# Output projections in 512-column weight tiles over half of the contraction, two banks per token block

## The chip, the cores and the metric

The kernel runs on one core of one Trainium2 chip. The metric is the device time of one launch in microseconds. Three runs of the kernel before gave 2868.2, 2872.81 and 2876.31 us, median 2872.81.

## What is computed

Four transformer layers over 512 tokens of width 1024, all in float32. The first two are a dilated window mixer and a differential attention mixer; the last two are each a hybrid mixer (indexer-selected attention beside gated linear attention) and a feed-forward network with a convolution of width 3. Cut to what matters here:

```
def dilated_mixer(h, w_in, w_out):          # layer 1; diff_mixer, layer 2, ends the same way
    ...
    y = o.reshape(B, S, DIL_WIDTH).astype(h.dtype) * jax.nn.silu(gate)
    return y @ w_out                        # 512x1024 @ 1024x1024: l1o, l2o

def hybrid_mixer(x, pos, ...):
    ik = partial_rope(ik[:, :, None, :], pos)[:, :, 0, :]      # the keys' rope
    ...
    merged = jax.nn.sigmoid(gate_a) * ya + jax.nn.sigmoid(gate_b) * yb
    return merged @ w_out + b_out           # m0o, m1o

def conv_ffn(x, w_up, conv_w, conv_b, w_down):
    ...
    return (jax.nn.gelu(a) * b) @ w_down    # contraction 2816 = 1024 + 1024 + 768: d0, d1, d2

h = h + rmsnorm(y, norm_post[i])            # first two layers: "resid"
x = layer_norm(DN_ALPHA * x + y, g, b)      # hybrid and feed-forward: "ln"
```

## The kernel before

**Split operands.** Every float32 operand of a projection is held as two fp32r parts, high and low, and a product is three matmuls: high x high, high x low, low x high. A weight tile arrives by DMA in one of two raw buffers (`WR`), in two halves; ScalarE writes its high part (step `split`, L1897) and POOL subtracts it for the low part in four pieces (step `lo`, L2821; the very first tile is done by VectorE in two). A tile is loaded when the low part of the tile two before it is done. The parts lie in one of three ring slots (`WS`), or, for the third tile of an output projection, in a fourth slot `EX`.

**Tiles.** 214 tiles are used in a fixed order. A name tells the stage (`l1`, `l2`: the first two layers; `m0`, `m1`: the hybrid mixers; `f0`, `f1`: the feed-forward networks) and the projection. "Token-major" products have the activations (in `UT` or `AT`) as stationary operand (L1552, "WS,UT" and so on); "feature-major" ones have the weights (L1549). The wide input projections use pairs of tiles of 512 columns, each over half the contraction (`-` marks the first half). The output projections `l1o`, `l2o`, `m0o`, `m1o` and the last part `f0d2`, `f1d2` use four tiles of 256 columns over the whole contraction (8 or 6 blocks of 128).

**One order for all engines.** The class `Order` writes out, ahead of the run, one list of steps; every engine walks that list in order and does its own part of each step, so each engine's queue has the order of the list. `fill(n)` puts the `split` steps of the tiles below n there, `tick` counts matmul steps: each tick pops one waiting `lo` and lets steps planned with `soon` (turns, ropes, splits) come when their count is over. `turn` is the transpose of one block of 128 tokens (TensorE, then ScalarE's high part and VectorE's low part); `wide(..., fresh=True)` is the first projection after a seam, which forces the turns it needs.

**The output projections.** `by_blocks` walks the four token blocks. Block 0 is opened by hand (list `opening`) while the last gates are transposed in chunks, and has four banks; the others have two banks of which each tile fills half. After a block its epilogue step follows: `resid` (ScalarE squares, VectorE, POOL's rstd, VectorE) or `ln` (VectorE, with POOL's rstd at L2836). The order is block by block, all four tiles in each. Then the next stage starts: `l2a0` after `l1o`, `m0iq` after `l2o` and `m1iq` after `f0d2` (both begin at token block 1), the feed-forward network's convolution table and its first pair after `m0o` and `m1o`.

**At a tile.** A product step waits, before its first matmul in the first block, for both halves of the high part and the whole low part.

Of the kernel before, what the change touches and what calls it, by code (L numbers as in the profile page):

```python
# [9 lines left out]
ALU = mybir.AluOpType  # L10
# [80 lines left out]
def weight_tiles(ap):  # L91
# [9 lines left out]

    out = []
# [9 lines left out]
    for j in range(4):  # L112
        out.append((f"l1o{j}", KC, 256, [(0, cols(ap["dil_w_out"][0], 256 * j))]))
# [6 lines left out]
    for j in range(4):  # L120
        out.append((f"l2o{j}", KC, 256, [(0, cols(ap["diff_w_out"][0], 256 * j))]))
    for l in range(2):
# [18 lines left out]
        for j in range(4):  # L141
            out.append((f"m{l}o{j}", KC, 256, [(0, cols(ap["w_mix_out_2"][l], 256 * j))]))
        for kind, j in ffn_order():
# [4 lines left out]
            elif j < 2:  # L148
                for c in range(2):
                    wide(f"f{l}d{j}{c}", ap["w_down_2"][l], 512 * c, r0=j * 1024)  # L150
            else:
                for c in range(4):
                    out.append((f"f{l}d{j}{c}", 6, 256, [(0, cols(ap["w_down_2"][l], 256 * c, k=6, r0=j * 1024))]))
# [19 lines left out]
class Order:  # L173
# [103 lines left out]
    def by_pool(self, i):  # L277

        return i > 0
# [56 lines left out]
    def wide(self, name, deal, by=1, fresh=False, hold=lambda: False, first=0):  # L336
# [42 lines left out]
    def by_blocks(self, names, finish, opening, order=(0, 1, 2, 3)):  # L379
# [3 lines left out]
        more = i0 + 4 < len(self.tiles)  # L383
        for b in range(NB):
            split = b == 0
            banks = (order, (4, 5), (0, 1), (2, 3))[b]
            for n, what in enumerate(opening if split else ()):
                if n == 2:
                    self.fill(i0 + 3)
                elif n == 4:  # L390
# [3 lines left out]
                else:  # L394
# [6 lines left out]
            for j in range(4):  # L401
                if len(ws) == j:
                    ws.append(self.open(names[j]))
                if not split or j == 3:
                    self.bank[ws[j], b] = (banks[j], 0) if split else (banks[j // 2], 256 * (j % 2))
                    self.step("mm", ws[j], b, 0, self.tiles[ws[j]][1])
                if b == 3 and j < LOOK and more and self.place[i0 + 4] < NS:
# [3 lines left out]
                if b == 1 and j < LOOK and more and self.place[i0 + 4] > NS:  # L411
# [2655 lines left out]
```

## Time and profile before

| | us |
|---|---|
| median of three runs | 2872.81 |
| the profiled execution | 2872.07 |
| its span, first to last instruction | 2870.8 |
| TensorE busy | 2765.1 |
| VectorE busy | 1196.3 |
| ScalarE busy | 1096.9 |
| POOL busy | 1115.2 |

The mean granted TensorE clock is 0.99 of full speed. PE is TensorE's matmuls, PEld its weight loads, DVE VectorE, ACT ScalarE, SP the queue that issues the DMAs. A row of the timeline says when a group of instructions began, how long it lasted, and in brackets how long the engine was idle before it and what ended that; the chain of work is followed back from the last instruction.

### The profile page before, as it was taken

What the parts mean: (1) busy time and instruction counts of PE and PEld (TensorE: products, weight loads), DVE (VectorE), ACT (ScalarE), POOL (GpSimd) and SP (SyncE); (2) the same over time, 40 slices, a digit from 0 to 9 for tenths busy, and PEclk for the clock granted to TensorE, in tenths of its full rate; (3) what the DMA queues carried; (4) which work ended last, traced back from release to release, by engine and by line L of the source; (5) the groups of instructions that cost most, each with busy time, mean ns of one, the idle gap of its engine ahead of it and who ended that gap; (6) DMA issues with size and microseconds to landing.
All of it is one profiled execution on the core that took longest, in us unless ns stands there. A gap on an engine that the chain in (4) does not pass through costs nothing.

```text
span 2870.8 us, 39675 instructions
## 1 busy us (share of the span) xinstructions
PE 2765.1 (96%) x15257; PEld 2278.5 (79%) x15257; DVE 1196.3 (42%) x2661; ACT 1096.9 (38%) x2045; POOL 1115.2 (39%) x902
## 2 busy tenths in 40 slices
PE   6999999998999999999999999989999999999998
PEld 5787878888878977776789888887777678988887
DVE  3333433344455355433335424255643433542425
ACT  3444434443455334362323424233436232342421
POOL 3323233334343343332355444434333235444443
PEclk9999999999999999999999999999999999999999
DMA  5332323232222142223253323224222324333331
GB/s 160 93 93 73 90 82 87 77 101 86 74 66 67 55 135 74 74 85 110 65 173 112 103 89 102 90 60 135 74 74 85 111 72 169 109 103 95 96 92 55
DMA packets 252670, 269.04 MB, mean 94 GB/s; under 512 B 16830, under 2 KB 214050, under 8 KB 251716
## 3 DMA queue, kind: packets, MB, share of 16 engines
q1 hardware_dynamic: 252484, 266.51, 30.4%
q8 instruction: 122, 2.00, 0.3%
q14 instruction: 64, 0.52, 0.1%
HBM read 247.52 MB, written 18.94 MB: 93 GB/s over the span
## 4 chain that ended last, share of the span: by engine, by line
PE 88%; DVE 6%; ACT 3%; issue 2%; POOL 1%; DMA 0%; SPq 0%; DVEq 0%; ACTq 0%; POOLq 0%
PE banks L1552 46%; PE banks L1549 27%; DVE AR L2239 2%; PE banks L1686 2%; PE banks L1570 2%; PE banks L1635 1%; PE banks L1793 1%; POOL WS L2821 1%; PE banks L1669 1%; PE banks L1706 1%; ACT WS L1897 1%; PE banks L1841 1%; PE banks L1609 1%; PE banks L1757 1%; PE banks L1654 1%
## 5 line engine op out<-in xcount | busy, mean ns | idle before, releaser
L2821 POOL TENSOR_TENSOR WS<-WR,WS 128x512 fp32r<-128x512 f32 (+2 forms) x812 | 1014.5, 1283 | 1460.7 <-ACT WS L1897 1460.7
L1552 PE MATMUL banks<-WS,UT 128*128 128x512 f32 (+1 forms) x5712 | 1210.5, 361 | 15.1 <-issue 7.0
L1552 PEld LDWEIGHTS banks<-WS,UT 128*128 128x128 f32 x5712 | 913.2, 190 | 190.5 <-issue 55.9
L1549 PE MATMUL banks<-UT,WS 128*128 128x512 f32 (+1 forms) x2832 | 667.8, 394 | 0.7 <-ACT AR L2072 0.7
L1549 PEld LDWEIGHTS banks<-UT,WS 128*128 128x128 f32 (+1 forms) x2832 | 528.6, 188 | 125.6 <-issue 15.4
L1897 ACT ACTIVATE WS<-WR 128x1024 fp32r<-128x1024 f32 (+2 forms) x408 | 396.0, 1021 | 203.3 <-PE banks L1552 151.2
L1552 PE MATMUL banks<-WS,AT 128*128 128x256 f32 (+1 forms) x1776 | 307.9, 334 | 13.1 <-issue 11.4
L1552 PEld LDWEIGHTS banks<-WS,AT 128*128 128x128 f32 x1776 | 267.9, 192 | 49.0 <-issue 12.1
L2239 DVE TENSOR_TENSOR AR<-AR 128x256 f32<-128x256 f32 (+2 forms) x173 | 157.5, 929 | 12.0 <-ACT AR L2140 7.2
L2761 DVE SCALAR_TENSOR_TENSOR AR<-banks,AR 128x511 f32<-128x511 f32 x84 | 63.0, 750 | 219.2 <-ACT AR L2208 219.2
L2836 POOL TENSOR_TENSOR SM<-SM 128x1 f32<-128x1 f32 (+2 forms) x44 | 47.0, 1069 | 275.5 <-DVE SM L2737 111.4
L2239 DVE TENSOR_TENSOR AR<-banks,CT 128x256 f32<-128x256 f32 (+1 forms) x168 | 71.9, 479 | 121.0 <-ACT AR L1965 64.9
L1951 ACT ACTIVATE AR<-banks 128x256 f32<-128x256 f32 (+1 forms) x118 | 59.3, 559 | 152.6 <-PE banks L1635 152.6
L2239 DVE TENSOR_TENSOR AR<-AR,banks 128x512 f32<-128x512 f32 (+1 forms) x72 | 43.6, 626 | 175.1 <-PE banks L1552 174.3
L2341 DVE CUSTOM_DVE_ANT_0 AF<-banks,MF 128x256 f32<-128x256 f32 (+1 forms) x128 | 47.0, 404 | 167.0 <-PE banks L1654 117.3
L2208 ACT ACTIVATE AR<-banks,AR 128x512 f32<-128x512 f32 x84 | 65.0, 774 | 87.9 <-PE banks L1549 81.7
L1549 PE MATMUL banks<-AT,WS 128*128 128x512 f32 x384 | 88.2, 391 | 0.0
L1549 PEld LDWEIGHTS banks<-AT,WS 128*128 128x128 f32 x384 | 72.1, 188 | 15.8
L1918 ACT ACTIVATE UT<-banks 128x512 fp32r<-128x512 f32 x48 | 26.2, 595 | 149.8 <-PE banks L1609 149.8
L2218 ACT ACTIVATE AT<-AR 128x512 fp32r<-128x512 f32 x40 | 25.3, 632 | 108.8 <-DVE AR L2239 108.8
L1686 PEld LDWEIGHTS banks<-AR,AF 128*128 128x128 f32 x480 | 61.7, 191 | 4.3 <-issue 0.7
L1984 ACT ACTIVATE AF<-banks 128x512 f32<-128x512 f32 (+1 forms) x64 | 36.7, 573 | 73.9 <-PE banks L1669 73.9
(220 smaller groups left out, 2647.0 us busy)
## 6 DMA issues: line engine op xcount, KB each, us to landing
WR<-in_w_in SPq DMA_DIRECT2D x112, 512.0 KB, 3.6
WR<-in_w_up SPq DMA_DIRECT2D x88, 512.0 KB, 3.6
WR<-in_dil_w_in SPq DMA_DIRECT2D x256, 128.0 KB, 2.5
WR<-in_w_down SPq DMA_DIRECT2D x32, 512.0 KB, 3.3
WR<-in_dil_w_in SPq DMA_DIRECT2D x16, 512.0 KB, 4.4
WR<-in_diff_w_in SPq DMA_DIRECT2D x32, 256.0 KB, 3.0
WR<-in_diff_w_in SPq DMA_DIRECT2D x16, 512.0 KB, 3.7
spill<-AR SPq DMA_DIRECT2D x32, 256.0 KB, 2.1
```

Source lines behind the costliest of these rows:

```text
L1549: mm = pe.matmul(B[bank][0:c, :], w[x][:, kk, g * P:g * P + c], act[:, y, kk, :], start=start, stop=stop)
L1552: mm = pe.matmul(B[bank][:, off:off + n], act[:, x, before_k + kk, g * P:g * P + P], w[y][:, kk, :], start=start, stop=stop)
L1570: mm = pe.matmul(B[c][:, 256 * half:256 * half + 256], w[x][:, kk, (c % 2) * P:(c % 2) * P + P], UT[:, y, kk, 256 * half:256 * half + 256] ...
L1686: mm = pe.matmul(B[ob][:, r:r + 64], fat(7168 + 512 * e + 256 * hh + j * P, P), vj, start=(j == 0), stop=(j == w // P - 1))
L1897: se.activation(slot(i, 0)[:, v * h:v * h + h], raw(i)[:, v * h:v * h + h], ACT.Copy).then_inc(hi.sem, 1)
L1951: se.activation(d, s, ACT.Copy).then_inc(pair_out.sem, 1)
L2208: se.activation(d, B[order.bank[i, half][0]][:, :], ACT.Identity, scale=cp[:, 2, f:f + 1], bias=cp[:, 3, f:f + 1]).then_inc(conv_id.sem, 1)
L2239: return ve.tensor_tensor(out_, x, y, op)
L2341: x = ve.tensor_tensor_reduce(P1(e, hh, w), B[4 + hh][:, 0:w], MF[:, 256:512] if far else MF[:, 256 - w:256], -0.125, -GONE, ALU.add, ALU. ...
L2761: ve.scalar_tensor_tensor(d[:, 1:T], bank[:, 0:T - 1], cp[:, 1, f:f + 1], d[:, 1:T], ALU.mult, ALU.add).then_inc(dve_step, 1)
L2821: ge.tensor_tensor(slot(i, 1)[:, s], raw(i)[:, s], slot(i, 0)[:, s].bitcast(F32), ALU.subtract).then_inc(lo_p.sem, 1)
L2836: ge.tensor_tensor(SM[:, o:o + n], SM[:, o:o + n], SM[:, MHALF:MHALF + n], ALU.pow).then_inc(rstd.sem, 1)
```

## The change

1. The output projections' tiles (`joined`) are 512 columns wide over 4 blocks of the contraction: tiles 0 and 1 are the first half, for the left and right columns, tiles 2 and 3 the rest (4 blocks, or 2 in `d2`). Each token block has two banks, block 0 too, and each bank collects two tiles.
2. `by_blocks` has a new order: block 0, block 1, then tiles 0 and 1 of blocks 2 and 3 (`(2,0),(3,0),(2,1),(3,1)`), then tiles 2 and 3 of block 2, its epilogue, tiles 2 and 3 of block 3, its epilogue. The third and fourth tiles are split before the first and second part of the opening; in `d2` the splits come around the last feature tile, and `d2`'s fourth tile gets its low part from VectorE.
3. Every product step makes its three passes one after another over its blocks of the contraction (weights high by activations high, high by low, then low by high), and waits for each half of the tile by itself: for the high half before, for the low half only before the third pass.
4. The partial rope (`part`, `small_tokens`) takes 4 VectorE instructions instead of 6, and the keys' rope 4 instead of 24 for its four blocks.
5. `m0iq` and `m1iq` alternate the two tile halves from token block 1 on.
6. At the start x's first block, the gain and the identity are loaded ahead of the first weight tile, x's second block behind it, and the second tile is split before x's third block is normalised.

```
+    def joined(name, w, r0=0, rest=4):
+        for half, k in enumerate((4, rest)):
+            for c in range(2):
+                out.append((f"{name}{2 * half + c}", k, 512, [(0, cols(w, 512 * c, 512, k=k, r0=r0 + 512 * half))]))
...
-        return i > 0
+        return i > 0 and self.tiles[i][0][2:] != "d23"
...
-            walk = [(half, b) for half in range(2) for b in (first, first + 1)]
-            walk += [(half, b) for b in range(first + 2, NB) for half in range(2)]
+            both = first + 2 if first == 0 else first
+            walk = [(half, b) for half in range(2) for b in range(first, both)]
+            walk += [(half, b) for b in range(both, NB) for half in range(2)]
...
-    def by_blocks(self, names, finish, opening, order=(0, 1, 2, 3)):
+    def by_blocks(self, names, finish, opening, first=(0, 1)):
...
+        banks_of = (first, (4, 5), (0, 1), (2, 3))
+        walk = [[], [(1, j) for j in range(4)],
+                [(2, 0), (3, 0), (2, 1), (3, 1), (2, 2), (2, 3)], [(3, 2), (3, 3)]]
...
-                if n == 2:
+                if n == 0:
                     self.fill(i0 + 3)
-                elif n == 4:
+                elif n == 2:
                     self.fill(i0 + 4)
...
-                    self.bank[ws[j], b] = (banks[j], 0)
+                    self.bank[ws[j], b] = (banks[j % 2], 0)
                     self.step("mm", ws[j], b, k0, k1)
-                    self.tick()
+                    self.tick((k1 - k0) // 2)
+            for g, j in walk[b]:
+                self.bank[ws[j], g] = (banks_of[g][j % 2], 0)
+                self.step("mm", ws[j], g, 0, self.tiles[ws[j]][1])
...
-        parts = [(0, 0, 4), (1, 0, 4), (0, 4, 6), (1, 4, 6), (2, 0, 6), (0, 6, 8), (1, 6, 8), (2, 6, 8)]
-        for n, what in enumerate(turns):
-            parts.insert(2 * n, what)
+        parts = [(0, 0, 4), (1, 0, 4), (2, 0, 2), (3, 0, 2), (2, 2, 4), (3, 2, 4)]
+        for n, what in zip((0, 2, 3, 5), turns):
+            parts.insert(n, what)
...
+            if b == 1:
+                self.fill(2)
...
                 i = self.open(f"f{l}b10")
+                self.fill(i + 4)
...
+                self.fill(i + 5)
...
-        self.by_blocks([f"f{l}d2{c}" for c in range(4)], finish, [(j, 0, 6) for j in range(3)], order=(2, 3, 0, 1))
+        self.by_blocks([f"f{l}d2{c}" for c in range(4)], finish,
+                       [(0, 0, 4), (1, 0, 4), (2, 0, 2), (3, 0, 2)], first=(2, 3))
...
+                    fetched = 0 if 2 * last <= k else 1
+                    opens = g == order.first_block.get(i, 0) and (first == 0 or 2 * first == k)
+                    if opens:
+                        pe.wait_ge(hi.sem, hi.at[i, fetched])
                     if first == 0:
-                        if g == order.first_block.get(i, 0):
-                            pe.wait_ge(hi.sem, hi.at[i, 1])
-                            pe.wait_ge(*lo_done(i))
...
-                    for kk in range(first, last):
-                        for q, (x, y) in enumerate(PASSES):
+                    for part, other in ((0, 0), (0, 1), (1, 0)):
+                        if part and opens:
+                            pe.wait_ge(*lo_done(i, fetched))
+                        for kk in range(first, last):
...
-                    for b in range(nb):
-                        x1, x2 = y[:, b, :, 0:8], y[:, b, :, 8:16]
...
-                        tt(q[0], x1, cs, ALU.mult)
-                        tt(q[1], x2, sn, ALU.mult)
-                        tt(q[2], x2, cs, ALU.mult)
-                        tt(q[3], x1, sn, ALU.mult).then_inc(dve_step, 1)
...
+                    tt(xc, x, cs.unsqueeze(2).to_broadcast([P, n, 2, 8]), ALU.mult)
+                    tt(xs, x, sn.unsqueeze(2).to_broadcast([P, n, 2, 8]), ALU.mult).then_inc(dve_step, 1)
+                    ve.wait_ge(dve_step, V.of())
+                    tt(x[:, :, 0, :], xc[:, :, 0, :], xs[:, :, 1, :], ALU.subtract)
+                    tt(x[:, :, 1, :], xc[:, :, 1, :], xs[:, :, 0, :], ALU.add).then_inc(done.sem, 1)
...
-            load_tile(0)
-            sy.dma_start(fat(2048, D), whole(ap["norm_pre"][0])).then_inc(gain_in, 16)
             x_by_rest = ap["x"][0].rearrange("(l r) d -> r l d", r=4)
             sy.dma_start(x_at[:, 0, :], x_by_rest[0]).then_inc(x_in[0], 16)
+            sy.dma_start(fat(2048, D), whole(ap["norm_pre"][0])).then_inc(gain_in, 16)
             sy.dma_start(IDN, tab[:, C_ID:C_ID + 128]).then_inc(id_in, 16)
-            for b in range(1, NB):
+            load_tile(0)
+            sy.dma_start(x_at[:, 1, :], x_by_rest[1]).then_inc(x_in[1], 16)
+            load_tile(1)
+            for b in range(2, NB):
```

## Rows read from the trace of the kernel before

**Rows 1.** The page's head and its busy times.

```profile
span 2870.8 us, 39675 instructions
...
PE 2765.1 (96%) x15257; PEld 2278.5 (79%) x15257; DVE 1196.3 (42%) x2661; ACT 1096.9 (38%) x2045; POOL 1115.2 (39%) x902
```

**Rows 2.** Chain of work: start us, us, what and how many.

```profile
978.96 11.06 PE banks L1552 x96
...
1542.67 11.47 PE banks L1552 x96
...
1657.87 44.80 PE banks L1552 x192
...
2513.36 76.18 PE banks L1549 x336
```

**Rows 3.** Timeline, the start: start us, us, engine, line [idle before].

```profile
13.40 1.06 ACT L1910 ACTIVATE AF<-AF 128x1024 f32<-128x1024 f32 x1 [11.39 <-DMA AF<-in_x]
...
16.99 1.94 PE L1609 MATMUL banks<-CT,AR 128*128 128x128 f32 x8 [16.99 <-DVE AR L2269]
...
19.46 1.99 ACT L1897 ACTIVATE WS<-WR 128x1024 fp32r<-128x1024 f32 x2
...
23.00 2.90 PE L1552 MATMUL banks<-WS,UT 128*128 128x512 f32 x6 [4.07 <-DVE WS L2239]
...
39.42 9.81 PE L1552 MATMUL banks<-WS,UT 128*128 128x512 f32 x42 [0.19 <-DVE UT L2239]
```

**Rows 4.** Timeline, openings of l1o, l2o, m0o and f0d2.

```profile
646.01 0.97 PE L1552 MATMUL banks<-WS,AT 128*128 128x256 f32 x6 [1.26 <-DVE AT L2239]
...
958.75 2.39 PE L1552 MATMUL banks<-EX,AT 128*128 128x256 f32 x18 [0.91 <-issue]
...
1514.88 8.86 PE L1552 MATMUL banks<-WS,UT 128*128 128x256 f32 x72 [0.87 <-issue]
...
1896.29 1.56 ACT L1897 ACTIVATE WS<-WR 128x768 fp32r<-128x768 f32 x2
...
1901.14 7.04 PE L1552 MATMUL banks<-WS,AT 128*128 128x256 f32 x36 [5.16 <-issue]
```

**Rows 5.** Timeline, the seam from l1o to l2a0.

```profile
689.56 10.92 POOL L2821 TENSOR_TENSOR WS<-WR,WS 128x512 fp32r<-128x512 f32 x8
...
691.99 1.09 PE L1609 MATMUL banks<-CT,AR 128*128 128x128 f32 x8 [0.98 <-DVE AR L2269]
...
695.62 12.54 PE L1552 MATMUL banks<-WS,UT 128*128 128x512 f32 x48 [2.53 <-issue]
...
700.43 0.56 POOL L2836 TENSOR_TENSOR SM<-SM 128x1 f32<-128x1 f32 x1
...
714.26 0.63 PE L1635 MATMUL banks<-CT,AR 128*128 128x128 f32 x4 [3.84 <-DVE UT L2239]
714.64 4.59 PE L1552 MATMUL banks<-WS,UT 128*128 128x512 f32 x12
```

**Rows 6.** Timeline, the keys' rope in the first hybrid mixer.

```profile
1030.20 3.94 DVE L2239 TENSOR_TENSOR SM<-AR 128x8 f32<-128x8 f32 x4 [6.59 <-ACT AR L2084]
...
1041.02 1.06 PE L1747 MATMUL banks<-CT,AR 128*64 128x128 f32 x4 [3.12 <-DVE AR L2239]
1041.73 5.31 PE L1552 MATMUL banks<-WS,UT 128*128 128x512 f32 x12
```

**Rows 7.** Timeline, the seam from f0d2 to m1iq.

```profile
1930.51 2.25 DVE L2745 SCALAR_TENSOR_TENSOR AR<-AR,SM 128x1024 f32<-128x1024 f32 x1 [0.51 <-POOL SM L2836]
...
1936.43 11.42 PE L1552 MATMUL banks<-WS,UT 128*128 128x512 f32 x42 [2.53 <-issue]
```

**Rows 8.** Timeline, the convolution table after m0o.

```profile
1556.08 0.41 PE L1865 MATMUL banks<-CT,AR 44*128 44x44 f32 x4 [1.07 <-DVE UT L2239]
```

**Rows 9.** Timeline, VectorE after the last matmul.

```profile
2862.77 0.69 DVE L2239 TENSOR_TENSOR AR<-AR,banks 128x512 f32<-128x512 f32 x1 [2.38 <-PE banks L1552]
```

**Rows 10.** Busy times of a stretch; the granted clock is PEclk.

```profile
core 0: us, PE busy (x) PEld busy (x) DVE busy (x) ACT busy (x) POOL busy (x), PEclk, DMA share, GB/s
1900.00:1908.00 8.00, 6.86 (x36) 6.89 (x37) 2.57 (x6) 0.00 (x0) 1.55 (x3) 0.57 0.40 131
```

More of the change, by code:

```diff
@@ L111, in weight_tiles @@
         out.append((f"l1g{j}", KC, 256, [(0, cols(w, 9216 + 256 * j))]))
-    for j in range(4):
-        out.append((f"l1o{j}", KC, 256, [(0, cols(ap["dil_w_out"][0], 256 * j))]))
+    joined("l1o", ap["dil_w_out"][0])
     w = ap["diff_w_in"][0]
@@ L119, in weight_tiles @@
         out.append((f"l2g{j}", KC, 256, [(0, cols(w, 3072 + 256 * j))]))
-    for j in range(4):
-        out.append((f"l2o{j}", KC, 256, [(0, cols(ap["diff_w_out"][0], 256 * j))]))
+    joined("l2o", ap["diff_w_out"][0])
     for l in range(2):
@@ L140, in weight_tiles @@
             out.append((f"m{l}pg{j}", KC, 256, [(0, cols(ap["p_gla_2"][l], 256 * j))]))
-        for j in range(4):
-            out.append((f"m{l}o{j}", KC, 256, [(0, cols(ap["w_mix_out_2"][l], 256 * j))]))
+        joined(f"m{l}o", ap["w_mix_out_2"][l])
         for kind, j in ffn_order():
@@ L151, in weight_tiles @@
             else:
-                for c in range(4):
-                    out.append((f"f{l}d{j}{c}", 6, 256, [(0, cols(ap["w_down_2"][l], 256 * c, k=6, r0=j * 1024))]))
+                joined(f"f{l}d{j}", ap["w_down_2"][l], r0=j * 1024, rest=2)
     return out
@@ L397, in by_blocks @@
                         ws.append(self.open(names[j]))
-                    self.bank[ws[j], b] = (banks[j], 0)
+                    self.bank[ws[j], b] = (banks[j % 2], 0)
                     self.step("mm", ws[j], b, k0, k1)
-                    self.tick()
[L401 to L407, printed above, removed]
+                    self.tick((k1 - k0) // 2)
+            for g, j in walk[b]:
+                self.bank[ws[j], g] = (banks_of[g][j % 2], 0)
+                self.step("mm", ws[j], g, 0, self.tiles[ws[j]][1])
+                if g == 3 and j < LOOK and more and self.place[i0 + 4] < NS:
                     self.limit += 1
@@ L1525, in tensor @@
                             pe.wait_ge(*before[i, g])
[L1526 removed]
+                    before_k = 4 if is_second(i) else 0
+                    if g == 0 and grouped[i]:
                         if name[:3] in ("l1o", "l2o"):
[L1528 removed]
+                            pe.wait_ge(chunk_lo.sem, chunk_lo.at[name[:2] + "g", before_k + last - 1])
                         elif name[0] == "m":
[L1530 to L1531 removed]
+                            pe.wait_ge(merge_lo.sem, merge_lo.at[int(name[1]), before_k + last - 1])
+                        elif before_k == 0:
                             pe.wait_ge(prod_lo.sem, prod_lo.at[int(name[1]), 9, 1])
@@ L1534, in tensor @@
                             pe.wait_ge(prod_lo.sem, prod_lo.at[int(name[1]), 10, 1, 0])
-                    if g == 2 and name[:4] in ("f0d2", "f1d2"):
+                    if g == 2 and grouped[i] and name[0] == "f" and is_second(i):
                         pe.wait_ge(prod_lo.sem, prod_lo.at[int(name[1]), 10, 1, 1])
```

71 lines of the change are left out of this document (27 added, 44 removed).

## The prediction

> **What bounds the kernel now.** I read the page first. TensorE is busy 96% of a span of 2870.8 us [rows 1], and no other engine comes near it. So only two things can move the time: how long one matmul takes, and the stretches in which TensorE stands still or runs at half clock. The idle left over is 105.7 us (2870.8 less 2765.1).
>
> The chain of work that ended last gives the matmul's price in dense stretches [rows 2]. A feature-major tile costs 76.18/336 = 0.2267 us per 512-column matmul; a token-major one whose stationary operand lies in AT costs 44.80/192 = 0.2333. The 256-column matmuls of the output projections cost 11.06/96 = 0.1152 us (stationary in AT, `l1o`) and 11.47/96 = 0.1195 (in UT, `m0o`). These are close to streaming time; there is nothing large to win in them.
>
> Then the timeline around every seam between two stages, where the bracket behind a PE row is its idle. The seams are: the start [rows 3], the openings of the six output projections [rows 4], the end of `l1o` into `l2a0` [rows 5], the keys' rope in the hybrid mixer [rows 6], `f0d2` into `m1iq` [rows 7], the convolution table [rows 8] and the tail [rows 9]. Behind the long idles the granted clock falls: 0.57 over 1900 to 1908 [rows 10], which is the lower of the two levels, 1.2 GHz, for most of the stretch. So an idle of 3 to 5 us is paid again in part.
>
> **The change, part by part.**
>
> *Wider matmuls.* 4 x 384 + 2 x 288 = 2112 matmuls of 256 columns become 1056 of 512. One token block (a quarter of a projection): `l1o`, `l2o`: 11.06 becomes 48 x 0.2333 = 11.20, +0.14, eight blocks +1.1. `m0o`, `m1o`: stationary in UT, where the 512-column price is nearest 0.2267: 11.47 becomes 10.88, eight blocks -4.7. `f0d2`, `f1d2`: 72 x 0.1152 = 8.29 becomes 36 x 0.2333 = 8.40, eight blocks +0.9. Sum **-2.7**. Were the price 0.2333 everywhere it would be 0; were it 0.2267 everywhere -7. The Trainium skill ("TensorE: Matmul & The Clock Gate", Back-to-back issue gap) gives N/2.4 + 2.5 ns for one isolated matmul; by that two of 256 cost 218.3 ns and one of 512 costs 215.8, and the whole would be an estimated -2.6 us. The rows say 230 to 239 against 227 to 233, so they keep the sum but not the sign in every stage.
>
> *Openings.* Block 0 now starts with four chunks in two banks, the third and fourth tiles are split earlier, and each half of a tile is waited for by itself, the low part only before the third pass. `l1o` idles 1.26 (waiting for a chunk's low part), `l2o` 0.91, `m0o` 0.87 (`m1o` repeats it) [rows 4]; three more idles like these, of 0.53, 0.44 and 0.52, lie beside them in `l1o` and `l2o`. In `l1o` ScalarE's two splits, 2.0 us each, now stand ahead of the chunk copies; I leave 0.6 us of idle in each. Gain 1.8 + 1.9 - 1.2 = 2.5, and 2 x 0.9 = 1.8 for `m`. For `f0d2` ScalarE splits the fourth tile only at 1896.29, POOL's four subtractions follow, and TensorE idles 5.16 us until 1901.14; then 36 matmuls take 7.04 instead of 36 x 0.1152 = 4.15, because the clock is low: 2.9 more [rows 4, 10]. After: the fourth tile (half as large per row) is split as soon as the last feature tile is done, its low part is on VectorE (0.7 us per half, as for the 512-wide addition of [rows 9]), and TensorE needs it 7 us (24 + 6 matmuls) after the opening. I leave 0.4. Gain 2 x (4.8 + 2.9) = 15.4. Together **-19.7**.
>
> *Seam `l1o` to `l2a0`.* TensorE idles 0.98 (a normalised block for the transposes), 2.53 (low part of the first tile; POOL subtracts from 689.56 to 700.48) and 3.84 (the rope of `l2a0`, late because POOL's rstd of block 3, which ends the previous stage, was queued behind those subtractions until 700.43) [rows 5]. At half clock 48 matmuls took 12.54 instead of 10.88 and 12 took 4.59 instead of 2.72: 3.5 us. Now the first two tiles of the projection end 16.8 and 11.2 us before its last matmul, so the next tiles' splits and subtractions (2.0 and 5.2 us each) are over before the seam, and rstd is not behind them. Blocks 2 and 3 finish only 24 matmuls = 5.6 us apart instead of 11; VectorE needs about 3 + 1.3 + 1.3 us a block, so block 3 is turned in time for its use 11 us into `l2a0`. Full gain 10.9; I take **-10**, and -5 for the range if the rope still waits.
>
> *Keys' rope.* 24 small VectorE products start at 1030.20 (the first four take 3.94 us) and end with the wait of TensorE, which idles 3.12 us until 1041.02 and then pays 5.31 for 12 matmuls instead of 2.72 [rows 6]; the second layer repeats it with 2.39 and 4.49 - 2.72 = 1.77. Four products with the blocks joined remain. They took 10.8/24 = 0.45 us each; at that they end 9 us earlier. At 1.4 us each (one POOL subtraction, 10.92/8 = 1.37 [rows 5], in front of every one) they still end at 1036, before TensorE asks at 1037.9. **-9.9.** The Trainium skill ("SBUF — State Buffer", SBUF: two separate sides) says a VectorE instruction with two SBUF inputs and a GpSimd one exclude each other for a whole instruction; the trace agrees in kind (four products spread over 3.94 us while POOL subtracts), and by it the bound is this same 1.4 us a piece.
>
> *Convolution table.* Its transposes come right after `m0o`'s last block, whose turn used to hold the bank. 1.07 idle in each of two layers [rows 8] goes: **-1.9** (rounded down by the switch).
>
> *The start.* x's first block is issued behind eight weight loads and a gain and reaches ScalarE at 13.40; the transposes start 3.6 us after that, the split of the tile at 19.46, the first product at 23.0; the fourth block's last stretch at 39.42 [rows 3]. After: x is first, so it lands near 5; the gain bounds the product, transposes near 8.5; the tile lands near 10.5, the first product near 12. Then blocks 2 and 3 of x come behind two weight tiles; ScalarE's order (norms 0, split, norm 1, split, norms 2 and 3, turn 1) puts block 1's turn near 22 instead of 30, and the same 4.1 us per block follow. **-8**; bounds -3 (bound by the loads) and -12.
>
> *What it costs.* In `m1iq` the walk starts at block 1 and alternates halves, so block 2's turn is needed after 24 matmuls and 8 transposes, 6.6 us after the seam. In VectorE's queue that turn's low part stands behind both `ln` of blocks 2 and 3, which now finish only 12 matmuls = 2.8 us apart. One `ln` is two additions (0.69 [rows 9], overlapping a little), two statistics of 0.64, 0.36 for two small ones, a product of 1.28, 0.5 of waiting for rstd and a last product of 1.28, or 2.25 beside POOL [rows 7]: 6 to 7 us. So: block 2 from -2.8 to +3, block 3 to +9.5, low part to +10.8: a new idle of 3.2 to 5.2, with half clock behind it (1.7) and 0.8 for a second late turn. It replaces 2.53 + 1.9 [rows 7]. **+2.0**. In `m0iq` the residual is shorter, only the second turn shows: **+0.8**. At the end VectorE does block 3 behind block 2: from the last matmul at 2862.7 it now takes about 8.4 instead of 5.3 us to the output: **+2.9** [rows 9].
>
> Sum: -2.7 - 19.7 - 10 - 9.9 - 1.9 - 8 + 2.0 + 0.8 + 2.9 = **-46.5**. The profiled execution took 2872.07 (span 2870.8 and 1.3 around it), 0.7 below the median 2872.81. So 2825.6 for such an execution, **2826** for the median.
>
> **Rivals.**
> - *A. The waits move, half the gain stays* (0.14). Two banks per block mean blocks 2 and 3 end together, and VectorE and ScalarE get their epilogues in a heap. If that costs an idle of 4 us with low clock in `l2a0` and `m0iq` too, and the start gains only 3: 2826 + 5 + 6 + 5 + 4 = 2846. For it: VectorE's queue in [rows 7]. Against: residual blocks are shorter than `ln`.
> - *B. More than I count* (0.12). The low part's later wait also helps wherever a split is late, and the start gains 12: 2808 to 2816. Against: the other waits of TensorE are for ropes and exponentials.
> - *C. Slower: the added waits break the stream* (0.04). 208 tiles get three more places at which TensorE waits in the middle of an accumulation: 624. If each opened a gap of 0.1 us, as long as the step from a 256-column product to another kind of operation shows (0.20 instead of 0.12 us in the records), it costs 62 us: 2888. It decides from 74 ns each. Against: 336 matmuls over seven tiles, with waits at each tile and bank, stay at 0.2267 [rows 2].
> - *D. No change: the new order of passes* (0.03). Now each product loads another stationary block, where before two of three shared one. If 6400 matmuls went from 0.2267 to 0.2333: +42 us, about 2868. Against: the shared and the unshared third are in the same 0.2267, 13 ns above 512/2.4.
> - My forecast: 0.67.
>
> The forecast's own range is 2816 to 2836; with A and B it is 2808 to 2848, which leaves out C, D and tails. No change means within 0.3% (8.6 us), which is about what can be told here. Faster 0.94, same 0.02, slower 0.04.
>
> **What would show it.** TensorE's first 512-column product near 12 us and the long run at 39.42 some 8 us earlier; no idle over 1.5 us at the opening of `f0d2` and `f1d2`; none before `l2a0` and the keys' transposes, and no fall of the clock there; a wait on VectorE's turn of 3 to 5 us in `m1iq`; last matmul to end of span 11 us instead of 8.3; 512-column products of `m0o` at 0.227 and of `l1o` at 0.233. I am wrong if dense stretches change their price, if the idle at the seams comes back under VectorE's name, or if the first tile is held up by the loads.

## The result, and the profile after

The changed kernel took 2833.82 us (median of four runs, 2832.68 to 2834.95) against 2870.51 for the kernel before beside it (2867.95 to 2876.31): ratio 0.9869, 95% interval 0.9852 to 0.9887. Between the two profiled executions the span went from 2870.8 to 2831.4 us, **39.4 less**; 46.5 were forecast. Line numbers of kernel.py have moved: L1552 is now L1562, L1549 is L1559, L1609 is L1619, L1635 is L1645, and VectorE's L2239 is L2249. In the kernels of the experiments the same lines have moved by a few more.

The head of the page, against [rows 1]: TensorE is busy 13.4 us less, and its idle has gone from 105.7 to 79.7 us.

```profile
span 2831.4 us, 37369 instructions
...
PE 2751.7 (97%) x14201; PEld 2220.0 (78%) x14201; DVE 1181.5 (42%) x2569; ACT 1095.8 (39%) x2037; POOL 1112.0 (39%) x894
```

The chain of work, against [rows 2]: the dense stretches have not changed their price by a hundredth. New are the 512-column products of the output projections, 16.71/72 = 0.2321 in `l1o` and 22.04/96 = 0.2296 in `m0o`.

```profile
643.73 16.71 PE banks L1562 x72
...
1486.00 22.04 PE banks L1562 x96
...
1560.09 76.18 PE banks L1559 x336
1636.27 44.80 PE banks L1562 x192
```

The following table compares the moments at which the same tile's first matmul starts in the two traces. Each line is the change in us of the distance between two such moments. The forecast's terms are grouped to the same places: of the 2.5 us for the openings, 1.2 stand at `l1o` and 1.3 at `l2o`, and of the matmuls' +1.1, half at each.

| from - to | forecast | measured |
|---|---|---|
| start to the second tile (the second half of `l1a0`) | -8.0 | -5.3 (42.3 to 36.9) |
| `l1o` to `l2v0`: opening, seam | -10.7 | -6.5 (86.2 to 79.7) |
| `l2o` to `m0ik` | 0.0 | -1.8 (71.3 to 69.5) |
| the keys' rope, two layers | -9.9 | -10.2 |
| `m0o`, `m1o` to the feed-forward network | -8.4 | -4.2 (76.2 to 74.1, twice) |
| `f0d2` to `m1ik`: opening, seam | -5.2 | -6.7 (67.9 to 61.2) |
| `f1d2` to the last matmul | -7.2 | -7.9 |
| last matmul to the end | +2.9 | +3.1 (8.3 to 11.5) |
| everywhere else | 0 | 0 (within 0.1) |
| sum | -46.5 | -39.5 |

Timeline, the start, against [rows 3]: the first product comes at 12.37 instead of 23.00, as forecast, but then TensorE stands 3.26 us for VectorE's low part of block 1, and works at the lower level of the clock, 1.2 GHz, behind it (6 matmuls in 2.93 us; the granted clock from 24.4 to 27.3 is 0.50).

```profile
12.37 2.93 PE L1562 MATMUL banks<-WS,UT 128*128 128x512 f32 x6 [1.63 <-ACT WS L1907]
...
23.05 1.27 DVE L2249 TENSOR_TENSOR UT<-banks,UT 128x512 fp32r<-128x512 f32 x2
24.38 2.93 PE L1562 MATMUL banks<-WS,UT 128*128 128x512 f32 x6 [3.26 <-DVE UT L2249]
```

Timeline, the seam from `l1o` to `l2a0`, against [rows 5]: of the three idles the first two are gone (TensorE runs through from 684.31), POOL's rstd of block 3 is on time (687.34, ahead of the subtractions of 692.85), and yet the third idle is there as before, 3.85 us, with 9 matmuls in 3.64 us behind it. VectorE's rows say why. What TensorE waits for is named UT, the low part of the turn of block 3 (701.58). It stands in VectorE's queue behind the ropes of blocks 0 and 1, which write AR; the sums of the first rope take 2.56 us beside POOL's subtractions, those of the second 0.76.

```profile
687.34 0.55 POOL L2835 TENSOR_TENSOR SM<-SM 128x1 f32<-128x1 f32 x1 [1.72 <-DVE SM L2460]
...
692.85 6.25 POOL L2820 TENSOR_TENSOR WS<-WR,WS 128x512 fp32r<-128x512 f32 x4 [0.21 <-ACT WS L1907]
...
695.45 1.34 DVE L2249 TENSOR_TENSOR AR<-banks,CT 128x512 f32<-128x512 f32 x3
696.82 2.56 DVE L2249 TENSOR_TENSOR AR<-AR 128x256 f32<-128x256 f32 x2
699.52 1.35 DVE L2249 TENSOR_TENSOR AR<-banks,CT 128x512 f32<-128x512 f32 x3
700.90 0.76 DVE L2249 TENSOR_TENSOR AR<-AR 128x256 f32<-128x256 f32 x2
701.58 1.28 DVE L2249 TENSOR_TENSOR UT<-banks,UT 128x512 fp32r<-128x512 f32 x2
...
696.14 1.03 PE L1619 MATMUL banks<-CT,AR 128*128 128x128 f32 x8
696.93 1.64 PE L1562 MATMUL banks<-WS,UT 128*128 128x512 f32 x6
702.41 0.63 PE L1645 MATMUL banks<-CT,AR 128*128 128x128 f32 x4 [3.85 <-DVE UT L2249]
```

Timeline, the keys' rope, against [rows 6]: two products and two sums in 3.9 us instead of 24 instructions in 10.8; TensorE reaches the transposes at 1024.18 with no idle and a full clock behind (12 matmuls in 2.99).

```profile
1016.63 1.49 DVE L2249 TENSOR_TENSOR SM<-AR 128x64 f32<-128x64 f32 x2 [6.74 <-ACT AR L2094]
1018.15 2.44 DVE L2249 TENSOR_TENSOR AR<-SM 128x32 f32<-128x32 f32 x2
...
1024.18 0.60 PE L1757 MATMUL banks<-CT,AR 128*64 128x128 f32 x4
```

Timeline, behind `m0o`, against [rows 8]: the convolution table comes without a wait, but a new idle of 1.86 us follows. It ends with L2750, VectorE's copy of the table, which frees a bank; that copy is queued behind the `ln` of block 3 (its last product takes from 1537.78 to 1539.99).

```profile
1531.70 0.44 PE L1875 MATMUL banks<-CT,AR 44*128 44x44 f32 x4
...
1539.92 0.33 DVE L2750 COPY AR<-banks 128x176 f32<-128x176 f32 x1
1540.30 0.66 PE L1619 MATMUL banks<-CT,AR 128*128 128x128 f32 x4 [1.86 <-DVE AR L2750]
```

Timeline, the opening of `f0d2`, against [rows 4]: no idle. And the seam into `m1iq`, against [rows 7]: the forecast wait for a turn, 4.17 us, and 18 matmuls in 5.99 us instead of the 4.28 that they take at 1903.31.

```profile
1867.83 5.77 PE L1562 MATMUL banks<-WS,AT 128*128 128x512 f32 x24
1873.44 1.54 PE L1562 MATMUL banks<-EX,AT 128*128 128x512 f32 x6
1874.91 7.26 PE L1562 MATMUL banks<-WS,AT 128*128 128x512 f32 x30
...
1903.31 4.28 PE L1562 MATMUL banks<-WS,UT 128*128 128x512 f32 x18
...
1914.03 5.99 PE L1562 MATMUL banks<-WS,UT 128*128 128x512 f32 x18 [4.17 <-DVE UT L2249]
```

Timeline, VectorE in the tail, against [rows 9]: block 3's `ln` starts when block 2's ends (2822.80), not when its own products do.

```profile
2821.59 1.28 DVE L2744 SCALAR_TENSOR_TENSOR AR<-AR,SM 128x1024 f32<-128x1024 f32 x1 [0.51 <-POOL SM L2835]
2822.80 1.28 DVE L2249 TENSOR_TENSOR AR<-AR,banks 128x512 f32<-128x512 f32 x2
```

The granted clock, against [rows 10]: 0.79 on the mean of the two stretches of 8 us around the idles that stay, that is, the lower level for some 3.4 of the 8 us (an estimate from 0.79, with the levels at 0.5 and 1).

```profile
core 0: us, PE busy (x) PEld busy (x) DVE busy (x) ACT busy (x) POOL busy (x), PEclk, DMA share, GB/s
...
700.00:708.00 8.00, 5.59 (x22) 4.58 (x23) 2.83 (x7) 0.75 (x2) 0.00 (x0) 0.79 0.22 68
1912.00:1920.00 8.00, 5.97 (x20) 4.75 (x21) 2.93 (x7) 0.00 (x0) 2.23 (x3) 0.79 0.79 286
```

### The profile page after: what moved, and what is told of

It is laid out like the page before. It is cut to its first block, busy times and chain, and to the rows that moved or that the text cites. A ratio compares the mean times of both kernels' runs of the same rounds, so it can differ in the third digit from the quotient of the medians.

```text
span 2831.4 us, 37369 instructions
## 1 busy us (share of the span) xinstructions
PE 2751.7 (97%) x14201; PEld 2220.0 (78%) x14201; DVE 1181.5 (42%) x2569; ACT 1095.8 (39%) x2037; POOL 1112.0 (39%) x894
## 4 chain that ended last, share of the span: by engine, by line
PE 89%; DVE 5%; ACT 2%; issue 2%; POOL 1%; SPq 0%; DMA 0%; DVEq 0%; ACTq 0%
PE banks L1562 47%; PE banks L1559 27%; PE banks L1696 2%; DVE AR L2249 2%; PE banks L1645 1%; PE banks L1580 1%; PE banks L1803 1%; PE banks L1679 1%; PE banks L1595 1%; PE banks L1716 1%; PE banks L1851 1%; POOL WS L2820 1%; PE banks L1664 1%; PE banks L1767 1%; PE banks L1781 1%
## 5 line engine op out<-in xcount | busy, mean ns | idle before, releaser
L1562 PE MATMUL banks<-WS,UT 128*128 128x512 f32 (+1 forms) x5424 | 1204.5, 370 | 10.3 <-DVE UT L2249 8.6
L1562 PEld LDWEIGHTS banks<-WS,UT 128*128 128x128 f32 x5424 | 894.8, 190 | 195.7 <-issue 43.5
L1559 PE MATMUL banks<-UT,WS 128*128 128x512 f32 (+1 forms) x2832 | 668.7, 395 | 0.7 <-ACT AR L2082 0.7
L1559 PEld LDWEIGHTS banks<-UT,WS 128*128 128x128 f32 (+1 forms) x2832 | 529.5, 189 | 125.6 <-issue 15.4
L1907 ACT ACTIVATE WS<-WR 128x1024 fp32r<-128x1024 f32 (+1 forms) x408 | 396.9, 1023 | 210.2 <-PE banks L1562 167.7
L1562 PE MATMUL banks<-WS,AT 128*128 128x512 f32 x1296 | 308.2, 396 | 0.0
L1562 PEld LDWEIGHTS banks<-WS,AT 128*128 128x128 f32 x1296 | 242.6, 188 | 58.4 <-ACT WS L1907 0.7
L2249 DVE TENSOR_TENSOR AR<-AR 128x256 f32<-128x256 f32 (+2 forms) x173 | 156.0, 920 | 12.0 <-ACT AR L2150 7.2
L2249 DVE TENSOR_TENSOR AR<-banks,CT 128x256 f32<-128x256 f32 (+1 forms) x168 | 71.9, 479 | 121.0 <-ACT AR L1975 61.7
L2249 DVE TENSOR_TENSOR AR<-AR,banks 128x512 f32<-128x512 f32 x64 | 43.0, 685 | 167.1 <-PE banks L1562 165.8
L1559 PE MATMUL banks<-AT,WS 128*128 128x512 f32 x384 | 88.2, 391 | 0.0
L1559 PEld LDWEIGHTS banks<-AT,WS 128*128 128x128 f32 x384 | 72.1, 188 | 15.8
L2249 DVE TENSOR_TENSOR UT<-banks,UT 128x512 fp32r<-128x512 f32 x48 | 31.1, 685 | 84.7 <-ACT UT L1928 84.7
```

What stands on the lines that cost most here:

```text
L1559: mm = pe.matmul(B[bank][0:c, :], w[part][:, kk, g * P:g * P + c], act[:, other, kk, :], start=start, stop=stop)
L1562: mm = pe.matmul(B[bank][:, off:off + n], act[:, other, before_k + kk, g * P:g * P + P], w[part][:, kk, :], start=start, stop=stop)
L1907: se.activation(slot(i, 0)[:, v * h:v * h + h], raw(i)[:, v * h:v * h + h], ACT.Copy).then_inc(hi.sem, 1)
L2249: return ve.tensor_tensor(out_, x, y, op)
```

## The experiments

Where no other is named, times by place compare the profiled execution with that of the changed kernel, again by the first matmul of the same tile. The start differs from execution to execution: the second tile begins at 36.9 us in the changed kernel and at 36.5 to 37.7 in the seven other kernels that keep its start. Two more stretches that no edit touches differ by 1.5 to 1.9 us, one from the second tile to `l1o` and one inside the hybrid mixers. In the first, TensorE idles 1.55 us (between 610 and 617 us) in all of them, and works behind it at a granted clock of 1.00 in some (the changed kernel, 614 to 617) and of 0.50 in others (613.6 to 617.0 in the run with the rope's transposes later). So a gain is read at its place, not in the span.

### The waits and the order of passes alone

The kernel before, with part 3 of the change.

```
+                    for part, other in ((0, 0), (0, 1), (1, 0)):
+                        if part and opens:
+                            pe.wait_ge(*lo_done(i, fetched))
+                        for kk in range(first, last):
```

> The kernel before, with one part of the change alone: each product step makes its three passes one after another and waits for each half of a tile by itself, for the low half only before the third pass. My theory: dense stretches keep their price (336 feature-major matmuls in 76.18 us, 192 token-major ones in 44.80), because neither the other stationary block in each pass nor the 624 places with a wait costs anything. What is gained is part of the idles that wait for a low part: 2.53 us before m1iq and 5.16 at the openings of f0d2 and f1d2, a few us in all, and nothing at l2a0, where the rope ends the stretch whatever comes before it. Total 3 to 8 us less than before: about 2865. Rival C (each wait opens a gap of 74 ns or more): 2916 or more. Rival D (0.2333 us instead of 0.2267 for each matmul that now loads another block): about 2912.

Measured: 2860.81 us against 2869.67, ratio 0.9969 (0.9957 to 0.998): 8.9 us less, where 3 to 8 were expected. Chain of work of this kernel, the rows that [rows 2] show for the one before:

```profile
1524.09 11.47 PE banks L1555 x96
...
1575.45 76.19 PE banks L1552 x336
1651.63 44.80 PE banks L1555 x192
```

So neither a wait between the passes nor the other order costs anything: rivals C and D fall. Against the kernel before, the opening of `f0d2` (up to the transposes behind it) is 2.2 us shorter and `f1d2` to the last matmul 4.1; in `f0d2` TensorE idles 1.93 and 0.63 us instead of 5.16. From there to `m1iq` 2.8 us more are won, where TensorE had waited for the first tile's low part. The waits also give 1.9 us from `l2o` to `m0ik`, as much as the changed kernel gains there (1.8), where nothing was forecast, and 1.1 us in each of `m0o` and `m1o`.

```profile
1891.68 2.59 PE L1555 MATMUL banks<-WS,AT 128*128 128x256 f32 x12 [1.93 <-ACT WS L1900]
1894.90 0.58 PE L1555 MATMUL banks<-WS,AT 128*128 128x256 f32 x1 [0.63 <-POOL WS L2824]
```

At `l2a0` this kernel reaches the tile 3.7 us sooner than the kernel before, and has given 3.8 back by the next tile (it idles 2.73 and 4.57 us there): an idle that a later step ends can't be earned from before it.

### The rope alone

The kernel before, with part 4 of the change.

```
+                    tt(xc, x, cs.unsqueeze(2).to_broadcast([P, n, 2, 8]), ALU.mult)
+                    tt(xs, x, sn.unsqueeze(2).to_broadcast([P, n, 2, 8]), ALU.mult).then_inc(dve_step, 1)
+                    tt(x[:, :, 0, :], xc[:, :, 0, :], xs[:, :, 1, :], ALU.subtract)
+                    tt(x[:, :, 1, :], xc[:, :, 1, :], xs[:, :, 0, :], ALU.add)
```

> The kernel before with the new partial rope alone: four VectorE instructions for the keys' four blocks instead of 24, and four instead of six for a block of queries. My theory: the two waits of TensorE before the keys' transposes (3.12 and 2.39 us) go, with the half clock behind them: 6.0 and 4.3 us less at these two places, nothing elsewhere: 2860.5. Rival: part of what the changed kernel gained at this place comes from its other order of waits, and the rope alone gives half or less: 2865 or more.

Measured: 2860.51 us against 2869.67, ratio 0.9967 (0.9954 to 0.998). Against the kernel before, the two places are 6.0 and 4.2 us shorter, up to the first scores behind the keys' transposes, as in the changed kernel to 0.1. The term is the rope's alone.

### The output projections block by block again

```
-        walk = [[], [(1, j) for j in range(4)],
-                [(2, 0), (3, 0), (2, 1), (3, 1), (2, 2), (2, 3)], [(3, 2), (3, 3)]]
+        walk = [[]] + [[(b, j) for j in range(4)] for b in (1, 2, 3)]
```

> The changed kernel with the output projections walked block by block again (blocks 1, 2 and 3, all four tiles each); tiles, banks, openings, waits, rope and start stay as changed. It tells what the interleaved order of blocks 2 and 3 gives and costs. My theory: the order starts the next stage's splits early and lets rstd of block 3 past POOL's subtractions, worth some 5 us before l2a0; but it bunches the epilogues of blocks 2 and 3, which costs 3.1 us in the tail, 4.8 in m1iq and 1 in m0iq. So the tail shrinks from 11.5 to 8.4 us, the idle of 4.17 in m1iq goes in part, and the seam before l2a0 grows. Net between -6 and +6: 2834. Rival: the order is what made the seams cheap, they come back to the 2.53 and 3.84 us of idle that they had before the change, in l2a0 and m1iq both: 2834 + 10 = 2844.

Measured: 2833.53 us, ratio to before 0.9873 (0.9858 to 0.9887): the same as the changed kernel. By place: seam `l1o` to `l2v0` +5.3, `l2o` to `m0ik` -0.8, `f0d2` to `m1ik` -2.1, the two mixers' ends -0.3 and -0.4, tail 8.4 instead of 11.5. Behind `m0o` the table's old wait of 1.07 us is back in place of the new 1.86. The interleaved order pays at one seam and costs at all others. At the one seam it is what takes the early idles away. Block by block TensorE idles 0.91 and 2.75 us, both times for a normalised block, and the wait for UT stays too. The second of them is the queue that the forecast named: POOL begins eight subtractions at 683.25, block 3 asks for its rstd at 689.2, and gets it at 694.22.

```profile
685.68 1.09 PE L1618 MATMUL banks<-CT,AR 128*128 128x128 f32 x8 [0.91 <-DVE AR L2278]
...
694.22 0.54 POOL L2834 TENSOR_TENSOR SM<-SM 128x1 f32<-128x1 f32 x1
...
700.97 1.82 PE L1618 MATMUL banks<-CT,AR 128*128 128x128 f32 x8 [2.75 <-DVE AR L2278]
...
708.01 1.09 PE L1644 MATMUL banks<-CT,AR 128*128 128x128 f32 x4 [2.96 <-DVE UT L2248]
```

### The idle that stayed before `l2a0`'s rope

```
-            self.soon(4, lambda: self.step("pairs", i, unit, *where))
+            self.soon(8 if where == ("2", 0) else 4, lambda: self.step("pairs", i, unit, *where))
```

> The changed kernel with the transposes of l2a0's first rope (the step pairs) four steps later, so that in TensorE's queue they stand behind 24 more matmuls. It tests why 3.85 us of idle stay there. Theory of the queue and the bank: these transposes need the bank that the turn of block 3 holds until VectorE has read it, and that read stands in VectorE's queue behind the ropes of blocks 0 and 1; all that TensorE could do meanwhile was ready. Then the idle falls to 1 us or less and the half clock behind it goes too (9 matmuls in 3.64 us instead of 2.04): 5 us less, 2829. Rival (the turn of block 3 is itself late, as its norm is): the matmuls of block 3 wait instead for the same 3.85 us, and nothing is gained: 2834.

Measured: 2827.67 us, ratio to before 0.985 (0.9834 to 0.9867); this place is 5.5 us shorter, and 0.4 of that is given back before `l2o`. VectorE does its work in the same order; TensorE has 24 matmuls where it stood still, and the clock doesn't fall (1.00 from 698 to 708):

```profile
699.13 5.71 PE L1562 MATMUL banks<-WS,UT 128*128 128x512 f32 x24
705.13 1.66 PE L1562 MATMUL banks<-WS,UT 128*128 128x512 f32 x6 [0.29 <-DVE UT L2249]
706.62 0.60 PE L1645 MATMUL banks<-CT,AR 128*128 128x128 f32 x4
```

The bank held by the turn was the wait; the turn itself comes only 0.29 us late for its own use. No run takes POOL's subtractions from beside the first rope, so what those 1.8 us (2.56 less 0.76) add to the wait is not shown.

### One `ln` out of the way in `m1iq`

```
+            if b == 3 and late:
+                self.soon(late, lambda: finish(3, ws, banks_of[3]))
```

`late` is 4 in `f0d2`, and 0 elsewhere.

> The changed kernel with one step moved: in f0d2 the epilogue of block 3 (ln) stands behind the turn of block 2 in every engine's list, four steps later. It tests what the idle of 4.17 us in m1iq waits for. Theory of the heap: VectorE's low part of that turn is queued behind two ln of 6 to 7 us each; with one of them out of the way the turn comes in time, and only a shorter wait for the turn of block 3 is left (some 2 us, since its ln starts 1.3 us later). The clock does not fall (18 matmuls in 4.1 us instead of 5.99). Stage m1iq 2 to 5 us shorter: 2830. Rival: VectorE's whole work of the two blocks is the bound, and the wait only moves from the turn of block 2 to that of block 3, at the same length and with the same fall of the clock: 2834.

Measured: 2839.99 us, ratio to before 0.9892 (0.9877 to 0.9906): 6 us slower than the changed kernel. By `m1ik` the profiled execution has lost 6.6. Neither theory gave that. The first half of mine holds: the turn of block 2 comes at 1910.46 and TensorE's wait for it is 0.18 us. The second half left out what else waits for the moved `ln`. The turn of block 3 waits 2.67 us for it (some 2 expected), and then the spill of all four blocks to memory (step `keep`) can only start when the last `ln` is done; ScalarE, with its part of `pairs` now ahead of its part of the turn, waits for that transfer until 1926.66, and TensorE stands 7.38 us more.

```profile
1911.81 4.36 PE L1565 MATMUL banks<-WS,UT 128*128 128x512 f32 x18 [0.18 <-DVE UT L2252]
...
1919.27 0.65 PE L1622 MATMUL banks<-CT,AR 128*128 128x128 f32 x4 [2.67 <-DVE AR L2747]
1927.31 1.11 PE L1622 MATMUL banks<-CT,AR 128*128 128x128 f32 x4 [7.38 <-ACT AR L1964]
...
1926.66 0.60 ACT L1964 ACTIVATE AR<-banks 128x512 f32<-128x512 f32 x1 [14.39 <-DMA keep<-AR]
```

### The tail

```
+        if not more:
+            walk = [[]] + [[(b, j) for j in range(4)] for b in (1, 2, 3)]
```

> The changed kernel with the last projection alone, f1d2, walked block by block. It tests the term for the tail: from the last matmul to the end 11.5 us in the changed kernel, 8.3 before it. Theory: VectorE's ln of block 3 (2822.80 to 2828.7) starts late only because that of block 2, which ends as late, is before it; block by block it starts with its own last matmul, and the tail is 8.4 us: 2831. Rival: the order also saves TensorE time in f1d2 (the splits are all early there, so it should not), and what the tail wins is lost ahead of it: 2834.

Measured: 2829.33 us, ratio to before 0.9856 (0.984 to 0.9873); the last matmul starts at 2819.13 and the end is at 2827.5, 8.4 us instead of 11.5. The term is as forecast, and nothing is lost ahead of it.

### The start

```
+        def turn_x(b):
+            self.step("turn", "x", b)
+            self.turned_to[b] = True
+            if b < 3:
+                self.step("norm", "x", b + 1)
```

> The changed kernel with the norms of x's third and fourth block behind the turns of the second and third in the list. It tests why only 5.3 of the 10.6 us that the first product wins are left when the fourth tile step starts. Theory: TensorE waits 3.26 us at half clock for the low part of block 1's turn, which VectorE does at 23.05 because two norms, and ScalarE's part of them, are queued ahead of it. With the norms behind, block 1 comes near 21 instead of 24.4, and 2 to 3.5 us of it last: 2831. Rival: blocks 2 and 3 then come late in their turn (their norms need POOL's rstd, now behind its subtractions of 1.5 us each), and nothing or less is left: 2834 or more.

Measured: 2832.55 us, ratio to before 0.9864 (0.985 to 0.9879); the whole time is 1.3 us below that of the changed kernel, less than their intervals tell apart. The second tile begins at 35.8 us; the last run below has the same start, and there it begins at 34.9. Against the 36.5 to 37.7 of the kernels that keep the changed start this is 0.6 to 2.8 us, where 2 to 3.5 were expected. Block 1's wait is gone (12 matmuls in one row from 19.09 on), but 1.69 us of idle for the normalised block 3 takes part of its place: both mechanisms are there. The 2.48 us before block 1's transposes are 1.48 in the changed kernel and 1.49 in the last run, so they are this execution's own.

```profile
17.48 1.97 PE L1623 MATMUL banks<-CT,AR 128*128 128x128 f32 x8 [2.48 <-DVE AR L2283]
19.09 5.03 PE L1566 MATMUL banks<-WS,UT 128*128 128x512 f32 x12
...
30.33 1.09 PE L1623 MATMUL banks<-CT,AR 128*128 128x128 f32 x8 [1.69 <-DVE AR L2283]
```

### What covers the fourth tile at the openings of `f0d2` and `f1d2`

Three kernels: without the two early splits (the two `fill` lines), with the low part of the fourth tile on POOL (the last two lines), and with both.

```
-                self.fill(i + 4)
...
-                self.fill(i + 5)
...
-        return i > 0 and self.tiles[i][0][2:] != "d23"
+        return i > 0
```

> The changed kernel without the two early splits around the last feature tile ahead of f0d2 and f1d2: the third and fourth tiles are split where the opening puts them. d2's fourth tile still gets its low part from VectorE. It tests the largest term of the prediction, 2 x 7.7 us for the openings of f0d2 and f1d2. Theory: the early splits carry most of it; without them TensorE idles 2 to 4 us again at each of the two openings, with half clock behind: 8 us more in all, 2842. Rival: the separate waits (low part only before the third pass) and the order of the products (30 matmuls before the fourth tile is wanted) are what covers the splits, as the kernel before with those waits alone idled 2.2 instead of 5.2 us there: no more than 2 us more, 2836.

> The changed kernel with the low part of d2's fourth tile on POOL again, as before the change; its early split stays. It goes on from the run without the early splits, which lost nothing. What covers the fourth tile at the openings of f0d2 and f1d2? Theory now: the smaller tile (ScalarE 1.14 us instead of 1.56 for its two halves), the late demand for its low part, and VectorE, which has it done 2.2 us after the split began; POOL needs four subtractions of 0.7 us each. Then TensorE waits for POOL's last piece, 1 to 2 us at each of the two openings: 2836. Rival (late demand covers this too): no idle there, 2833.

> Both undone at once in the changed kernel: no early splits ahead of f0d2 and f1d2, and the low part of d2's fourth tile by POOL. The opening then has only the new tiles, the new order of products and the separate waits. Theory: as without VectorE alone, plus the 1.3 us by which the split is later: 2 to 3 us of idle at each opening, 2838. Rival: the separate waits and the order of products alone are enough, no idle: 2833.

Measured: 2833.11, 2837.87 and 2838.32 us; ratios to before 0.9867 (0.9853 to 0.9882), 0.9893 (0.9879 to 0.9906) and 0.9895 (0.9881 to 0.9908). The early splits are worth nothing: without them ScalarE splits the fourth tile at 1874.98, when TensorE has done two of the four tiles of block 0 (it entered `f0d2` at 1869.32), and TensorE runs through. That is 5.7 us after the entry; with the early splits it was 5.9 (1873.73, entry at 1867.83), for ScalarE's list is held up by the gates of the last feature tile either way.

With POOL, which takes 2.80 us for the low part against VectorE's 1.29 for both halves, TensorE idles 1.16 us at each opening, and each opening is 1.4 us longer (1.2 without the early splits as well). The whole times are 4.1 and 4.5 us longer. The rest doesn't lie at the openings. In the profiled execution with POOL alone 1.3 us of it lies in `m1iq`, where the granted clock is 0.50 for 6.8 us (1916.4 to 1923.2) instead of 3.4; no run shows that this comes from POOL.

The kernel without early splits, and the one with POOL:

```profile
1869.32 5.77 PE L1560 MATMUL banks<-WS,AT 128*128 128x512 f32 x24
1874.93 1.54 PE L1560 MATMUL banks<-EX,AT 128*128 128x512 f32 x6
...
1874.98 1.14 ACT L1905 ACTIVATE WS<-WR 128x512 fp32r<-128x512 f32 x2
...
1876.31 7.16 PE L1560 MATMUL banks<-WS,AT 128*128 128x512 f32 x30
```

```profile
1875.96 2.80 POOL L2820 TENSOR_TENSOR WS<-WR,WS 128x256 fp32r<-128x256 f32 x4 [5.23 <-ACT WS L1907]
...
1878.81 6.33 PE L1562 MATMUL banks<-WS,AT 128*128 128x512 f32 x26 [1.16 <-POOL WS L2820]
```

### Put together

The rope's transposes later, the interleaved order in `l1o` alone, and the start of the run above.

```
+        if names[0][:2] != "l1":
+            walk = [[]] + [[(b, j) for j in range(4)] for b in (1, 2, 3)]
```

> What the runs so far point to, together: the changed kernel with the transposes of l2a0's first rope four steps later, the interleaved order of blocks 2 and 3 kept in l1o alone and all other output projections walked block by block, and the start with the norms of x's last two blocks behind the turns. By the stages of the single runs: l2a0 -5.5, m0iq -0.8, m1iq -2.1 and the two mixers' ends -0.7 (block by block), tail -3.1, start -1.1: -13 from 2833.8, so about 2821. Rival (the stages are not independent: what one wait frees, the next takes): 2826 or more.

Measured: 2820.17 us, ratio to before 0.983 (0.9817 to 0.9844). By place: start -2.1, seam after `l1o` -5.5, `l2o` to `m0ik` -0.8, behind `m0o` -1.1 and `m1o` -0.8, `m1iq` -2.1, tail -3.1, together some -15.5. But the profiled execution is only 12.5 us shorter than that of the changed kernel: layer 1 is 1.5 us longer, the second hybrid mixer 1.3 (the two stretches named above that differ by themselves), and 0.4 follows the later transposes. The medians differ by 13.7 us, where 13 were expected: the stages add up within that scatter.

## Why the prediction was right or wrong

**The sum and its sign.** Right: 2833.8 lies in the range and in the forecast's own, 8 us above the likeliest value. The terms for the keys' rope (-9.9, measured -10.2), the tail (+2.9, +3.1), `f1d2` (-7.2, -7.9) and the cost in `m1iq` held, each at its place. Rivals B, C and D fell; C and D by a run of their own. The 624 places of rival C are 576 by the order of steps (three in each of 184 tiles and one in each of 24), which changes nothing in its fall. Of rival A one part is true: the idle of 4 us with the lower clock is there in `l2a0`; in `m0iq` TensorE stands only 0.83 us. Part of the nearness is luck: the start, the seam behind `l1o`, `m0o` and `m1o` gave 11.1 us less than forecast, while `l2o`, the rope, `f0d2` and `f1d2` gave 4.3 more. And one of the forecast's own signs of being wrong came true: at two seams the idle is back under VectorE's name.

**The seam `l1o` to `l2a0` is the step that failed: -10 stood there, the whole place with its opening gave -6.5.** I had put the idle of 3.84 us down to "the rope of `l2a0`, late because POOL's rstd of block 3 ... was queued behind those subtractions". The rstd did come earlier, as argued, and the idle stayed to a hundredth. The row itself [rows 5] names UT, what a turn writes, and not AR, what the rope writes. What was missing in the forecast was the bank: `pairs` needs the one that the turn of block 3 holds, and VectorE reads it only behind two ropes. The -5 that I kept for the range "if the rope still waits" was the case, by another mechanism. Later transposes give 5.5 us there, more than the 4.2 that were missing. The openings fell short a little too: TensorE idles 1.14 us in that of `l1o` and 0.79 in that of `l2o`, where 0.6 had been left for each.

**`m0o` and `m1o`: -4.2 forecast each, -2.1 measured.** Two terms. The 512-column product costs 0.2296 and not 0.2267 us: 48 x 0.0029 = 0.14 us in each of four blocks, 0.6 for each projection, inside the bounds that were kept. And the wait for the convolution table went, but its copy on VectorE, queued behind two `ln`, holds the bank of the next turn: 1.86 us of idle behind `m0o`, 1.52 behind `m1o`. I counted the wait removed and did not ask what the moved step makes late.

**The start: -8 forecast, -5.3 measured.** The first product is where it was said to be (12.37). Block 1's turn was put "near 22"; ScalarE does its part at 19.41, but VectorE's low part comes at 23.05 behind two norms, one of them stretched to 2.28 us beside POOL. It is the size that was off, by one queue that I had not followed to its end. The two runs with the norms moved show that 0.6 to 2.8 us of it can be had in this way.

**`f0d2` and `f1d2`: the size right, the cause half wrong.** "The fourth tile is split as soon as the last feature tile is done" was to bring it; removing that costs nothing. Each opening is 7.9 us shorter. The separate waits by themselves give 2.2 and 4.1 of it, and VectorE's low part 1.2 to 1.4 each. The rest, some 4 and 2 us by difference, is left for tile and order (the fourth tile is smaller and wanted late), which no run took away by themselves.

**The interleaved order.** I charged it with +2.0, +0.8 and +2.9 and credited it with the early splits before `l2a0`. The run block by block gives 2.1, 0.8 and 3.1 us for these places and 5.3 for the seam behind `l1o`: the forecast's prices were right, and the order as a whole is worth nothing, 2833.5 against 2833.8.

## What to carry to other kernels

Read what a wait's row says was written: it tells which step in the other engine's queue ends the wait, and a step that is on time can still be read late, or hold a bank, because it is queued behind work that nobody waits for. In a kernel with one order for all engines, putting an operation some steps later on the waiting engine can take the wait away without making its producer faster; here it gave 5.5 us. An order should be chosen for each seam: bunching two epilogues cost as much at the other seams here as it won at one. And when a wait is removed, look for the instruction that now stands at the end of that queue, its bank and its spill included.

## What the runs showed of the hardware that was not expected

A wait in the middle of an accumulation is free when it is already met: with 576 more such places 336 matmuls still take 76.19 us (76.18 before). Loading another stationary block for each matmul, where two of three in a row had used the same one, costs nothing either. The profile counts a weight load for every matmul before the change too (15257 of each), so this doesn't tell what fewer loads would be worth.

VectorE took 2.56 us for two sums of 256 columns, both inputs in AR, while POOL subtracted (692.85 to 699.10), and 0.76 us for two such sums after that. The Trainium skill ("SBUF — State Buffer", SBUF: two separate sides) says that a VectorE instruction with two SBUF inputs and a GpSimd instruction that reads SBUF exclude each other on their shared port for the whole instruction. The rows agree in kind, with a factor of 3.4 here.

A short idle of TensorE is not always paid twice. Behind the same idle of 1.55 us ahead of `l1o` the granted clock stayed at 1.00 (2.4 GHz) in some executions and was 0.50 (1.2 GHz) for 3.4 us in others; the time up to `l1o` differs by 1.5 us between the two kinds.
